# Sample attention with one product per head for the new tokens, and input, norm and key loads moved behind weight rows

## The reference, cut to what matters

```
k_all = concat([paged_rows(cache_k, page_table), ak_s])   # per sample 256 cached + 8 new keys
v_all = concat([paged_rows(cache_v, page_table), av_s])
attn_s = dsa_attend(aq_s, ..., k_all, v_all, ki_all, ...) # 8 heads of 128
...
logits = where(valid, q.k * scale + bias, -inf)           # only the selected keys
p = softmax(logits)
out = einsum('bhtj,btjhd->bthd', p, v_sel)                # sum over cached and new values
...
hs = hs + mixer_output(hm, mo, attn_s, mh_norm_g, w_out)  # w_out: 2048 x 2048
hs = hs + peer(rmsnorm(hs, norm2_g), peer_wq, k1, k2, U, V)
```

## Time and profile before

| | |
|---|---|
| Median of 3 runs | 2743.24 us (2741.44, 2743.24, 2760.86) |
| Profiled execution | 2737.79 us, its span 2735.9 us |
| PE busy | 2301.7 us (84%) |
| DVE busy | 1458.5 us (53%) |
| Read from HBM | 833.26 MB |
| First wait of POOL's gathers ends | 1027.11 us |

### The profile page before, as it was taken

One profiled execution on the slowest core, in us unless ns is written; L12 is line 12 of the kernel. 1 busy time (PEld: TensorE's weight loads), 2 busy tenths in 40 slices (PEclk: granted clock), 3 DMA queues, 4 the chain that ended last, 5 costly groups with the idle time before them and its releaser, 6 DMA issues.

```text
span 2735.9 us, 21188 instructions
## 1 busy us (share of the span) xinstructions
PE 2301.7 (84%) x7673; PEld 1264.8 (46%) x7673; DVE 1458.5 (53%) x2651; ACT 417.9 (15%) x879; POOL 379.7 (14%) x363
## 2 busy tenths in 40 slices
PE   4999999785689898999899999877877777777776
PEld 3999999543555343434344444322322232222221
DVE  4333333465620015656754455888888865555554
ACT  3222222321310010011200001211111100010000
POOL 0000000000010001221212222222222122222221
PEclk8999999866589899999999999999999999999999
DMA  4444443214035879999999999999999999999997
GB/s 128 148 128 134 142 151 119 76 56 114 1 119 183 287 264 408 418 373 426 389 421 425 416 404 420 413 415 421 407 414 422 424 417 428 428 428 428 428 429 298
DMA packets 159866, 844.78 MB, mean 309 GB/s; under 512 B 9862, under 2 KB 97730, under 8 KB 117274
## 3 DMA queue, kind: packets, MB, share of 16 engines
q0 software_dynamic: 46080, 671.11, 58.3%
q1 hardware_dynamic: 113706, 172.67, 19.0%
HBM read 833.26 MB, written 10.21 MB: 308 GB/s over the span
## 4 chain that ended last, share of the span: by engine, by line
PE 56%; DMA 27%; DVE 11%; issue 4%; ACT 1%; SPq 0%; DVEq 0%; POOL 0%; ACTq 0%; POOLq 0%
DMA rows_in<-in_peer_uv,expert 26%; PE bank L246 19%; PE bank L272 7%; PE bank L1025 5%; PE bank L1026 5%; PE bank L1027 5%; PE bank L259 4%; DVE rows_in L548 3%; PE bank L1002 1%; PE bank L1217 1%; PE bank L1207 1%; PE bank L1179 1%; DVE diag L523 1%; PE bank L1143 1%; PE bank L1132 1%
## 5 line engine op out<-in xcount | busy, mean ns | idle before, releaser
L246 PE MATMUL bank<-rows_in,diag 128*128 128x512 f32 (+1 forms) x2560 | 1189.0, 611 | 268.7 <-DVE diag L523 268.1
L548 DVE CUSTOM_DVE_ANT_0 rows_in<-rows_in,x2n 128x2048 f32<-128x2048 f32 x320 | 733.5, 2292 | 521.7 <-DMA rows_in<-in_peer_uv,expert 521.2
L246 PEld LDWEIGHTS bank<-rows_in,diag 128*128 128x128 f32 (+1 forms) x2560 | 451.9, 183 | 987.3 <-issue 546.0
L454 POOL DMA_INDIRECT rows_in<-in_peer_uv,expert x320 | 364.5, 1139 | 1509.4 <-PE bank L246 1301.0
L1025 PE MATMUL bank<-xnh,wh 128*128 128x336 f32 x896 | 285.8, 319 | 23.2 <-DVE wl L1448 23.2
L356 ACT ACTIVATE dots<-dots 128x1 f32<-128x1 f32 x320 | 64.9, 203 | 1507.8 <-DVE dots L548 1507.8
L1027 PE MATMUL bank<-xnh,wl 128*128 128x336 f32 x896 | 286.0, 319 | 0.0
L1026 PE MATMUL bank<-xnl,wh 128*128 128x336 f32 x896 | 285.6, 319 | 0.0
L1448 DVE TENSOR_TENSOR wl<-wring,wh 128x2048 fp32r<-128x2048 f32 x56 | 128.2, 2292 | 266.1 <-ACT wh L1271 266.1
L1025 PEld LDWEIGHTS bank<-xnh,wh 128*128 128x128 f32 x896 | 170.6, 190 | 24.0 <-issue 24.0
L1026 PEld LDWEIGHTS bank<-xnl,wh 128*128 128x128 f32 x896 | 170.5, 190 | 0.0
(11 more groups left out here) (288 smaller groups left out, 1517.3 us busy)
## 6 DMA issues: line engine op xcount, KB each, us to landing
wring<-in_w_in SPq DMA_DIRECT2D x28, 2048.0 KB, 8.2
wk<-in_w_out SPq DMA_DIRECT2D x64, 512.0 KB, 9.1
wk<-in_peer_wq SPq DMA_DIRECT2D x64, 512.0 KB, 8.7
kT<-in_keys_t SPq DMA_DIRECT2D x16, 512.0 KB, 5.5
vpage<-in_cache_v SPq DMA_DIRECT2D x16, 512.0 KB
rows_in<-in_peer_uv,expert POOLq DMA_INDIRECT x320, 12.4
C<-in_state_C SPq DMA_DIRECT2D x4, 1024.0 KB, 5.8
out_C_sample<-C SPq DMA_DIRECT2D x4, 1024.0 KB, 4.5
```

The source lines that it names most:

```text
L246: mm = pe.matmul(accs[t][d][0:w, :], diag[r % ND][:, 0:w], rows_in[r % NG][:, D + 512 * d:D + 512 * d + 512], start=False, stop=(j == ROUN ...
L454: nc.gpsimd.indirect_dma_start(out=rows_in[r % NG][:], out_offset=None, in_=UV_DR, in_offset=bass.IndirectOffsetOnAxis(ap=ids[:, j:j + 1], ...
L548: nc.vector.tensor_tensor_reduce(u, u, x2n[t][:], 1.0, 0.0, ALU.mult, ALU.add, dots[t % 2][:, j:j + 1]).then_inc(S["dot_done"], 1)
```

## The change

Samples' attention: the product with the 8 new values is taken out of the loop over samples. While DVE divides the probabilities, it writes those of the new tokens into `newS` (64 rows: head and token; 64 columns: sample and token), and the others back in place. After the last sample PE transposes `newS` once (bank "sQ"), DVE multiplies it per head with `same8` (ones where a row and a column are of the same sample) into `pzn`, a block-diagonal matrix of 64 x 64 per head, and PE does one product per head with all 64 new value rows, straight out of `av_nat`. `vnew`, its 8 loads, the third transposes and ACT's second copies go.

Loads: SP issues rows 6 to 15 of `w_out` directly after the first six, ahead of the wait for "sT2"; then `h1[0]`, rows 16 to 31, `g2`, rows 0 to 15 of `peer_wq`, `kT12`, rows 16 to 31, `h1[1]`, `h1[2]`, and `gf` as before. For the first 128 rows DVE waits for `xr_in` at 16 only.

```diff
+    jobs.append((("sQ",), lane % 6))
     jobs += [(("sO", 0), 6), (("sO", 1), 7), (("sT2",), 0)]
...
         weight_rows(a["w_out"][0], 0, range(NW))
...
+        weight_rows(a["w_out"][0], 0, range(NW, KC))
         evacuated(sp, ("sT2",))
-        for t in range(2):
-            sp.dma_start(h1[t][:], xp[P * t:P * t + P]).then_inc(S["xr_in"], 16)
+        sp.dma_start(h1[0][:], xp[0:P]).then_inc(S["xr_in"], 16)
+        weight_rows(a["w_out"][0], 0, range(KC, 2 * KC))
+        broadcast(g2, a["norm2_g"][0], "g2_in")
+        weight_rows(a["peer_wq"][0], 1, range(KC))
+        sp.dma_start(kT12[:], ...).then_inc(S["keys_in"], 16)
+        weight_rows(a["peer_wq"][0], 1, range(KC, 2 * KC))
+        sp.dma_start(h1[1][:], xp[P:2 * P]).then_inc(S["xr_in"], 16)
         for n in range(2):
             sp.dma_start(h1[2][TS * n:TS * n + TS, :], xs).then_inc(S["xr_in"], 16)
-        broadcast(g2, a["norm2_g"][0], "g2_in")
-        sp.dma_start(kT12[:], ...).then_inc(S["keys_in"], 16)
-        weight_rows(a["w_out"][0], 0, range(NW, 2 * KC))
-        weight_rows(a["peer_wq"][0], 1)
         broadcast(gf, a["final_norm_g"], "gf_in")
...
-            dve.wait_ge(S["xr_in"], 64)
+            dve.wait_ge(S["xr_in"], 64 if g else 16)
...
-        pz = at("pz", NR + 16896, [P, 3, AH, 2 * TS - ST])
+        pz = at("pz", NR + 16896, [P, 2, AH, 2 * TS - ST])
+        pzn = at("pzn", NR + 37000, [TS, AH, TS])
+        newS = at("newS", NR + 39048, [AH * ST, TS])
+        same8 = at("same8", NR + 39304, [TS, SB])
...
-                sp.dma_start(vnew[b % 2][:], av_nat[ST * b:ST * b + ST, 3, :]).then_inc(S[f"v_in{b % 2}"], 16)
...
-                    pe.wait_ge(S[f"v_in{n % 2}"], 48 * (n // 2 + 1))
+                    pe.wait_ge(S[f"v_in{n % 2}"], 32 * (n // 2 + 1))
                     for h in range(AH):
                         dst = outs[h // 4][0:TS, DH * (h % 4):DH * (h % 4) + DH]
                         for g in range(2):
                             mm = pe.matmul(dst, pz[:, g, h, ...], vpage[n % 2][:, g, h * DH:(h + 1) * DH], ...)
-                        mm = pe.matmul(dst, pz[0:ST, 2, h, ...], vnew[n % 2][:, h * DH:(h + 1) * DH], ...)
+                    mm.then_inc(S["sO_done"], 1)
...
-                    for j, (c, w) in enumerate(((0, P), (P, P), (PAST, ST))):
-                        mm = flip(b[0:w, j * AH * ST:(j + 1) * AH * ST], logitS[(q - 1) % 2][:, c:c + w], AH * ST)
+                    for j in range(2):
+                        mm = flip(b[:, j * AH * ST:(j + 1) * AH * ST], logitS[(q - 1) % 2][:, P * j:P * j + P], AH * ST)
+                    close(mm)
+                if q == SB:
+                    b = open_bank(("sQ",))
+                    close(flip(b[0:TS, 0:AH * ST], newS[:], AH * ST))
+            evacuated(pe, ("sQ",))
+            for h in range(AH):
+                mm = pe.matmul(outs[h // 4][0:TS, ...], pzn[:, h, :], av_nat[0:TS, 3, h * DH:(h + 1) * DH],
+                               start=False, stop=True, skip_group_check=True)
+                if h % 4 == 3:
                     close(mm)
...
-                    nc.scalar.copy(pz[:, 0:2, :, TS - ST:TS], ...)
-                    give(nc.scalar.copy(pz[0:ST, 2, :, TS - ST:TS], ...), ("sP", n))
+                    give(nc.scalar.copy(pz[:, 0:2, :, TS - ST:TS], ...), ("sP", n))
...
+            link(nc.vector.tensor_reduce(same8[:], ident[0:TS, 0:TS].rearrange("p (b t) -> p b t", t=ST), AX_X, ALU.add))
...
-                    nc.vector.tensor_scalar(logitS[n % 2][:], logitS[n % 2][:], top8S[...], None, ALU.mult).then_inc(S["probS_done"], 1)
+                    nc.vector.tensor_scalar(newS[:, ST * n:ST * n + ST], logitS[n % 2][:, PAST:KS], top8S[...], None, ALU.mult)
+                    nc.vector.tensor_scalar(logitS[n % 2][:, 0:PAST], logitS[n % 2][:, 0:PAST], top8S[...], None, ALU.mult).then_inc(S["probS_done"], 1)
+            b = take(dve, ("sQ",))
+            for h in range(AH):
+                ins = nc.vector.tensor_tensor(pzn[:, h, :].rearrange("p (n t) -> p n t", t=ST), ..., ALU.mult)
+            give(ins, ("sQ",))
```

More of the change, by code:

```diff
@@ L213, in tail_sync @@
         yp, ys = o["y_prompt"][0], o["y_sample"].rearrange("b t d -> (b t) d")
+        weight_rows(a["w_out"][0], 0, range(NW, KC))
         evacuated(sp, ("sT2",))
-        for t in range(2):
-            sp.dma_start(h1[t][:], xp[P * t:P * t + P]).then_inc(S["xr_in"], 16)
+        sp.dma_start(h1[0][:], xp[0:P]).then_inc(S["xr_in"], 16)
+        weight_rows(a["w_out"][0], 0, range(KC, 2 * KC))
+        broadcast(g2, a["norm2_g"][0], "g2_in")
+        weight_rows(a["peer_wq"][0], 1, range(KC))
+        sp.dma_start(kT12[:], a["keys"].rearrange("d (n k) -> d n k", n=2 * PH)).then_inc(S["keys_in"], 16)
+        weight_rows(a["peer_wq"][0], 1, range(KC, 2 * KC))
+        sp.dma_start(h1[1][:], xp[P:2 * P]).then_inc(S["xr_in"], 16)
         for n in range(2):
             sp.dma_start(h1[2][TS * n:TS * n + TS, :], xs).then_inc(S["xr_in"], 16)
-        broadcast(g2, a["norm2_g"][0], "g2_in")
-        sp.dma_start(kT12[:], a["keys"].rearrange("d (n k) -> d n k", n=2 * PH)).then_inc(S["keys_in"], 16)
-        weight_rows(a["w_out"][0], 0, range(NW, 2 * KC))
-        weight_rows(a["peer_wq"][0], 1)
         broadcast(gf, a["final_norm_g"], "gf_in")
@@ L743, in build @@
         kT = [at(f"kT{s}", o_, [P, AH, KS]) for s, o_ in enumerate((NR, 8192))]
-        pz = at("pz", NR + 16896, [P, 3, AH, 2 * TS - ST])
+        pz = at("pz", NR + 16896, [P, 2, AH, 2 * TS - ST])
         vpage = [at(f"vpage{s}", PR + s * 8192, [P, 2, AH * DH]) for s in range(2)]
-        vnew = [at(f"vnew{s}", NR + 32832 + s * 4096, [ST, AH * DH]) for s in range(2)]
+        pzn = at("pzn", NR + 37000, [TS, AH, TS])
+        newS = at("newS", NR + 39048, [AH * ST, TS])
+        same8 = at("same8", NR + 39304, [TS, SB])
         qpad = at("qpad", AV, [P, SB, AH * (TS + ST)])
@@ L1216, in _ @@
                         for g in range(2):
[L1217 to L1226, removed]
+                            mm = pe.matmul(dst, pz[:, g, h, TS - ST - ST * n:2 * TS - ST - ST * n], vpage[n % 2][:, g, h * DH:(h + 1) * DH],
+                                           start=(n == 0 and g == 0 and h % 4 == 0), stop=False, skip_group_check=True)
+                    mm.then_inc(S["sO_done"], 1)
                 if 1 <= q <= SB:
@@ L1229, in _ @@
                     pe.wait_ge(S["probS_done"], q)
-                    for j, (c, w) in enumerate(((0, P), (P, P), (PAST, ST))):
-                        mm = flip(b[0:w, j * AH * ST:(j + 1) * AH * ST], logitS[(q - 1) % 2][:, c:c + w], AH * ST)
+                    for j in range(2):
[6 more added lines that the diff above has]
+            for h in range(AH):
+                mm = pe.matmul(outs[h // 4][0:TS, DH * (h % 4):DH * (h % 4) + DH], pzn[:, h, :], av_nat[0:TS, 3, h * DH:(h + 1) * DH],
+                               start=False, stop=True, skip_group_check=True)
+                if h % 4 == 3:
                     close(mm)
@@ L1379, in _ @@
                         act.wait_ge(S["sO_done"], n)
-                    nc.scalar.copy(pz[:, 0:2, :, TS - ST:TS], b[:, 0:2 * AH * ST].rearrange("p (n h t) -> p n h t", n=2, h=AH))
-                    give(nc.scalar.copy(pz[0:ST, 2, :, TS - ST:TS], b[0:ST, 2 * AH * ST:3 * AH * ST].rearrange("p (h t) -> p h t", h=AH)), ("sP", n))
+                    give(nc.scalar.copy(pz[:, 0:2, :, TS - ST:TS], b[:, 0:2 * AH * ST].rearrange("p (n h t) -> p n h t", n=2, h=AH)), ("sP", n))
             for n in range(2):
@@ L1699, in _ @@
                     link(nc.vector.reciprocal(top8S[:, n % 2:n % 2 + 1], stS[:, 2 + n % 2:3 + n % 2]))
-                    nc.vector.tensor_scalar(logitS[n % 2][:], logitS[n % 2][:], top8S[:, n % 2:n % 2 + 1], None, ALU.mult).then_inc(S["probS_done"], 1)
+                    nc.vector.tensor_scalar(newS[:, ST * n:ST * n + ST], logitS[n % 2][:, PAST:KS], top8S[:, n % 2:n % 2 + 1], None, ALU.mult)
+                    nc.vector.tensor_scalar(logitS[n % 2][:, 0:PAST], logitS[n % 2][:, 0:PAST], top8S[:, n % 2:n % 2 + 1], None, ALU.mult).then_inc(S["probS_done"], 1)
+            b = take(dve, ("sQ",))
+            for h in range(AH):
+                ins = nc.vector.tensor_tensor(pzn[:, h, :].rearrange("p (n t) -> p n t", t=ST),
+                                              b[0:TS, ST * h:ST * h + ST].rearrange("p (a t) -> p a t", a=1).to_broadcast([TS, SB, ST]),
+                                              same8[:].rearrange("p (n a) -> p n a", a=1).to_broadcast([TS, SB, ST]), ALU.mult)
+            give(ins, ("sQ",))
             tail_vector(dve, link)
```

## The result

The changed kernel ran in 2707.73 us (median of 4 runs, 2700.46 to 2714.48); the kernel before in 2751.87 us (4 runs, 2741.44 to 2760.86). The ratio on record is 0.9849, 95% interval 0.9816 to 0.9882 (the quotient of these two medians is 0.9840): 1.5% faster, and 2707 was forecast. A second set on another chip gave 2710.63 against 2746.89 and again 0.9849 (0.9817 to 0.9880). In that set one run of the changed kernel (4086.83 us) and one of the kernel before (5829.02 us) stand far outside and are left out. The profiled execution took 2700.46 us, its span 2698.6.

The account below looks back on a forecast made before the run. PE's chain through the samples' attention and part 0 bounds the first gather's start. Attention -29.0 and part 0 -7.5 make -36.5 us on 2737.79: 2701.3, plus 5.45 for the median, 2707 us; range 2700 to 2719.

Parts of the forecast that it names:

- signs of being wrong: Passes staying 0.145 us apart, logits waiting for keys, rows behind `h1[0]` or `kT12` late, time after first gather growing.
- The step of the loop: Samples' attention: output as one stretch of 32 equal passes takes 3.66 us, saving 3.85 per sample, 30.8 for eight.
- rival (d): Passes in the samples' loop keep 0.145 us, so 7.7 us less are won, 2715 us; chance 0.08.
- rival (e): Weight loads and products of equal shape take turns, 0.25 us a pass; attention 7 us slower, 2743 us; chance 0.01.
- The end of the loop: After the last sample: one transpose and sixteen passes in 1.9 us, DVE's multiplies hidden; together +2.0 us.
- the small items: Samples' loop: third transpose, ACT's second copy and DVE's extra operation together give -0.5 us.
- The transfers of the loop: Keys land 7.6 us after an output ends, needed after 8.5, 0.9 left; sample 7's values cost 0.3 us.
- rival (b): Keys become the loop's bound: landing 3.9 us later, four samples wait 3 us each, +12, 2719 us; chance 0.09.
- Part 0: Its stall for row 6 and second slow stretch go, the first stays: 65.4 us becomes 57.9, -7.5 us.
- The moved loads: Loads placed between weight rows stay hidden: `h1[0]` and `kT12` with 0.9 us left, `g2` by 1.4 us at worst.
- rival (c): Weight rows stall once behind a moved load and the clock falls; the 7.5 us are not won, 2714; chance 0.11.
- hidden, and through before the gathers start: `h1[1]`, `h1[2]` ahead of part 2's first row: 4 MB take 10 us, about 17 us are there.

Follow-up runs that it names:

- regroup: Kernel before, with each sample's sixteen cached-value products first, then its eight new-value products; median 2729.3 us against 2747.86, ratio 0.9929.
- keys_early: Changed kernel with keys of sample b+2 issued before values of sample b; samples' attention 81.7 us, ratio to the kernel before 0.9845.
- spread: Changed kernel with `h1[1]` issued after 8 and `h1[2]` after 24 rows of `peer_wq`; median 2707.51 us, ratio 0.9846.
- both: Changed kernel with keys of sample b+2 before values of b, and `h1[1]`, `h1[2]` among `peer_wq` rows; median 2703.3 us, ratio 0.9833.
- inputs_late: Changed kernel with earlier keys, and `h1[1]`, `h1[2]`, `gf` issued behind the first six rows of part 2; median 2697.83 us, ratio 0.9832.
- before_again: The kernel before, unchanged, profiled once more; span 2742.8 us, samples' attention 122.4 us.

## Why the prediction was right

**The forecast and its sum.** 2707 against 2707.73, and -36.5 us against -37.5 in the touched stages. The mechanism held; that the number is hit within 1 us is luck. The attention gave 1.9 us less than forecast and parts 0 and 1 gave 2.9 us more, the clock's -7.9 and +7.0 in untouched stages cancelled, and the forecast started from a median of 2743.24 where the full set has 2751.87. Of the signs of being wrong that the prediction names, three came in small: logits waited for keys, rows behind the moved loads came up to 0.9 us late in some runs, and the time after the first gather was 7.0 us longer, which goes with the clock and not with the change.

**The step of the loop.** The main term, 30.8 us from 32 pass starts 0.11 us apart in one group, held: 7.52 - 3.64 is 3.88 us, 31.0 us for eight, and `regroup` shows its disputed half alone. The price of a pair of changes is 0.28 us (0.94 less six passes of 0.11), not the 0.25 that the text reads from the four passes; the sum did not use it. So rival (d) and rival (e), equal loads and products in turn, are both out. The Trainium skill ("TensorE: Matmul & The Clock Gate", Part 3, The mechanism) lets weight loads overlap running products only when the row groups differ, though the same section also names a background weight buffer. This trace speaks against the strict form: 32 loads of the same 128 rows within 3.47 us beside their 32 passes.

**The end of the loop and the small items** held: 1.90 us, DVE's multiplies hidden.

**The transfers of the loop.** This term was mis-sized. I took landing of keys at 7.6 us after the output's end and up to 0.1 us of wait per sample; it was 2.0 us in all (0.90 + 0.28 + 0.85), with the median landing at 6.8 instead of 5.5 us. The sum carried 0.3 us, for the values of sample 7, and none of the waits for keys; those values cost nothing. The rival (b) thus came true in small. The step that failed is the margin of 0.9 us, taken from one burst per 12 us: with a step of 8.2 us the bursts follow closer, and SP's wait for an output stood ahead of keys that could already go (`keys_early`).

**Part 0.** -8.7 against -7.5: the stall and the second slow stretch went, as argued, and the first slow stretch was shorter as well. The forecast kept it at seven passes; the profile after has four passes in 3.07 us at a clock of 0.52:

```profile
848.23:851.30 3.07, 3.07 (x4) 1.47 (x5) 1.02 (x2) 0.00 (x0) 0.00 (x0) 0.52 0.03 13
```

In the first run with earlier keys the same 128 passes took 55.17 us, with no slow stretch. Part 1, forecast unchanged, fell from 56.8 to between 55.1 and 56.2 in all versions with both parts of the change, except `spread` and `both` with three loads in it. Its slow start is gone; the first 3.6 us before and after:

```profile
956.20:959.80 3.60, 3.60 (x5) 1.53 (x6) 0.00 (x0) 0.00 (x0) 0.00 (x0) 0.50 0.00 0
913.68:917.28 3.60, 3.60 (x9) 1.69 (x10) 0.00 (x0) 0.00 (x0) 0.00 (x0) 1.00 0.11 25
```

Why it is gone stays open: the engine's wait just before is 0.87 us in both.

**The moved loads.** `h1[0]` cost 0 to 0.9 us, `kT12` 0 to 0.9, `g2` nothing: margins of about 1 us were right, and used up, and rival (c) came true in small. Wrong was "hidden, and through before the gathers start" for the 2 MB ahead of part 2: 4 MB in 10 us, within 17, were forecast from 409 GB/s. From the issue of `h1[1]` at 959.05 to the landing of the first row, when PE starts at 978.89, are 19.8 us, at 290 to 292 GB/s; `wk` rows landed up to 17.5 us after issue and the first came 3.84 us late. It cost nothing that shows at the end (`inputs_late`).

**The stages that were not to change.** The forecast set the whole sum against one profiled execution. That one had the clock at 1.00 in the outputs of samples 6 and 7. In three of four profiles of that loop it was at 0.50 there, which is 11.6 us more. So against most executions of the kernel before, the attention gains 38.7 us, not 27.1. A ratio of 0.9849 is 41 us, and such falls can be why it is not 37; the timed runs have no clock by stage, so that is argued and not shown (the two medians of the second set differ by 36.3). The new loop had no fall in eight profiles; which of its traits does it was not tried. It is not the alternation of shapes alone: `regroup`, which groups them, fell for 3 us, and in passes of one shape.

## What to carry to other kernels

Put products of one shape next to each other: between 128-row and 8-row weights each change cost 0.14 us here, more than a pass, and grouping alone was worth 14 us in its profile. When a loop gets shorter, look at what its queue waits for ahead of each load: a key load parked behind an unrelated wait was the next thing late. One 1 MB load between weight rows cost 0 to 0.9 us here; three within 28 us (932.4, 946.2 and 960.7 in `spread`) cost 6 us. And cut profiles of several executions at the same marks, with the granted clock beside them, before a difference of 7 us is given a cause; read every output's time, since a fall of 3 us hides in a stage's total.

## What the runs showed of the hardware

TensorE's granted clock fell to 0.50 in the middle of work: in `before_again` PE had been busy 12.55 of 13 us, with no wait above 0.5 us, in logits and in products of 64 x 128 that alternate between two row counts. It fell so in three of four profiles, and in the other was 1.00 there. In `regroup`, with products grouped by row count, it fell for 3 us. Two other stages go with the clock between executions of one kernel: the prompt's attention (102.4 us at a mean clock of 0.71, 112.1 at 0.62) and the 320 gathers (1709.1 and 1718.8). Changing the row count of consecutive f32 products cost 0.14 us a change at full clock.
